# Output projection, mixing, both norms and modulation token tile by token tile, row broadcasts beside the head norm, and six attention projections inside the rwkv scan

## The reference

```
u = LN(x) * (1 + scale1) + shift1
h = u @ w_in                      # columns split into the groups of three mixers
y = concat[ RWKV-7 both ways (4 heads x 64),
            differential attention with rotary q, k (4 heads, q/k 2x64, v 128),
            HGRN2 both ways (4 heads x 64) ] @ w_out
x = LayerNorm(alpha * x + gate1 * y)
x = LayerNorm(alpha * x + gate2 * PEER(LN(x) * (1 + scale2) + shift2))
```

## Time and profile before

| | us |
|---|---|
| median of 3 runs | 6208.47 (6203.03 to 6233.56) |
| the profiled execution | 6228.09 |
| its span, first to last instruction | 6226.5 |

### The profile page before, as it was taken

The page is one execution under the profiler, slowest core; times in us unless marked ns, Lnnn a source line. Parts: engine busy times, 40 slices in busy tenths (PEclk is TensorE's granted clock), DMA queues, the critical chain, the costliest instruction groups (busy, mean ns, idle before and its releaser), DMA issues.

```text
span 6226.5 us, 64675 instructions
## 1 busy us (share of the span) xinstructions
PE 5310.1 (85%) x22991; PEld 3572.5 (57%) x22991; DVE 3707.7 (60%) x8308; ACT 1464.0 (24%) x3638; POOL 1473.6 (24%) x1540
## 2 busy tenths in 40 slices
PE   8899888786787799999999589987796846999997
PEld 3699644554663455555555379944473745666664
DVE  1545252744886688887665465416373697775665
ACT  1100021312276412112111210003221165111111
POOL 0000000000024555445553000000000036434552
PEclk9899989678897799999999789998757956999998
DMA  6000000001357899999997100010001438999996
GB/s 219 21 1 1 24 17 27 8 20 62 119 197 274 346 418 414 401 405 404 399 413 299 49 4 1 1 37 7 31 1 42 141 123 328 415 418 412 417 417 272
DMA packets 292960, 1184.08 MB, mean 190 GB/s; under 512 B 24736, under 2 KB 106912, under 8 KB 207392
## 3 DMA queue, kind: packets, MB, share of 16 engines
q0 software_dynamic: 92160, 671.13, 26.4%
q1 hardware_dynamic: 194864, 455.59, 20.0%
q10 hardware_dynamic: 5616, 53.23, 2.1%
HBM read 1130.57 MB, written 49.28 MB: 189 GB/s over the span
## 4 chain that ended last, share of the span: by engine, by line
PE 65%; DVE 18%; DMA 10%; ACT 3%; issue 2%; POOL 2%; ACTq 0%; SPq 0%; DVEq 0%; POOLq 0%
PE psum L510 64%; DMA arena<-in_ut 6%; DVE arena L1376 3%; DMA arena<-gate_blocks 2%; DMA x_tokens<-in_uv,arena 1%; DVE arena L1706 1%; DVE arena L1515 1%; DVE arena L1781 1%; DVE arena L1385 1%; DMA arena<-in_uv,arena 1%; DVE arena L1513 1%; ACT arena L1001 1%; DVE arena L1379 1%; DVE arena L1587 1%; ACT y_features L1077 1%
## 5 line engine op out<-in xcount | busy, mean ns | idle before, releaser
L510 PE MATMUL psum<-arena 128*128 128x64 f32 (+7 forms) x8416 | 1550.1, 361 | 46.0 <-DVE arena L1706 23.9
L510 PE MATMUL psum<-u_features,weight_ring 128*128 128x256 f32 (+2 forms) x4672 | 1319.7, 439 | 36.7 <-ACT arena L1106 18.3
L510 PEld LDWEIGHTS psum<-arena 128*128 128x128 f32 (+2 forms) x8416 | 1082.8, 213 | 397.3 <-issue 279.5
L510 PEld LDWEIGHTS psum<-u_features,weight_ring 128*128 128x128 f32 x4672 | 896.7, 194 | 454.4 <-issue 240.0
L1354 POOL TENSOR_TENSOR arena<-consts 128x1 f32<-128x1 f32 x640 | 334.9, 523 | 1264.4 <-DVE y_features L1610 1092.3
L510 PE MATMUL psum<-u_features,arena 128*128 128x384 f32 (+1 forms) x2048 | 588.1, 442 | 39.3 <-DMA arena<-in_ut 35.6
L1001 ACT ACTIVATE arena<-psum 128x512 f32<-128x512 f32 (+5 forms) x404 | 250.6, 620 | 1543.1 <-PE psum L510 1313.2
L510 PE MATMUL psum<-weight_ring,consts 128*128 128x512 f32 x1280 | 570.3, 592 | 0.0
L510 PEld LDWEIGHTS psum<-u_features,arena 128*128 128x128 f32 x2048 | 396.7, 195 | 253.9 <-issue 56.5
L1355 POOL DMA_INDIRECT arena<-in_uv,arena x350 | 485.3, 1387 | 99.3 <-POOL arena L1354 93.5
L1112 ACT ACTIVATE arena<-arena 128x1 f32<-128x1 f32 x640 | 129.8, 203 | 1485.4 <-DVE arena L1602 1482.3
(11 more groups left out here) (201 smaller groups left out, 5437.2 us busy)
## 6 DMA issues: line engine op xcount, KB each, us to landing
weight_ring<-in_ws SPq DMA_DIRECT2D x250, 512.0 KB, 3.6
weight_ring<-in_ut SPq DMA_DIRECT2D x128, 512.0 KB
weight_ring<-in_uv SPq DMA_DIRECT2D x128, 512.0 KB
arena<-in_ut SPq DMA_DIRECT2D x128, 512.0 KB
arena<-in_uv SPq DMA_DIRECT2D x128, 512.0 KB
gate_blocks<-arena ACTq DMA_DIRECT2D x20, 2048.0 KB, 7.8
arena<-gate_blocks SPq DMA_DIRECT2D x32, 768.0 KB, 18.9
arena<-gate_blocks SPq DMA_DIRECT2D x32, 512.0 KB, 27.2
```

The lines of the kernel that those rows point to most:

```text
L510: return pe.matmul(o, w, x, start=first, stop=last, skip_group_check=True)
```

## The change

There are two parts.

**Attention pieces in the scan.** In pass i of the rwkv scan, 12 of the 14 filler slots no longer hold three identity matmuls but a part of the q/k projection of piece i: eight slots with one matmul of 128x512 (the latent tokens, into PSUM bank 3), and four with two matmuls of 128x256 (the context, into bank 7). ACT copies both results out in the same pass. Six of eight pieces are done so, and two remain in `project`. Their targets QA and KA can't lie in the arena during the scan, so they now lie in X. The tokens in X are overwritten by that and loaded again during the hgrn stage: in layer 0 from the inputs, in layer 1 from x_kept, where ACT stores them at the start of the layer.

**The tail of the mixers.** The rows of gate1 and of mod2 (the shift and scale of the second modulation) are broadcast right after the hgrn scan, during the head norm. Four of the eight pieces of w_out stay in the ring, the other four are loaded into the arena once the hgrn scan has left it, so that PE can project all 1024 columns of one tile before it goes to the next. Mixing, both norms, transposes and modulation follow tile by tile, with two PSUM buffers for the projection and two for the transposes. The first two query pieces, which need only the first two tiles, stand ahead of the last tile's transposes.

The diff, cut to its core:

```diff
-        QA, KA = take(4 * T), take(4 * T)
+        QA, KA = X[:, 0:4 * T], X[:, 4 * T:8 * T]
...
+        WO2 = [take(PIECE) for _ in range(WO // 2)]
+        G1 = [take(D) for _ in range(2)]
+        BC = [take(D) for _ in range(4)]
...
+                    if n == tokens_back_at(l) + WO // 2:
+                        for d in range(2):
+                            sp.wait_ge(*at("hgrn state", l, NT - 1, d))
+                        for c in range(WO // 2):
+                            sp.dma_start(WO2[c], a["ws"][pieces_before(DEPTH) + l * (WO // 2) + c]).then_inc(SEM["second_half_in"], 16)
...
+                    if n == tokens_back_at(l):
+                        sp.wait_ge(*at("attn scores", l, BH * len(tiles(l)) - 1, 1))
+                        if l == 0:
+                            load_tokens("x_again")
+                        else:
+                            sp.wait_ge(SEM["x_spilled"], 16 * 2 * l)
+                            sp.dma_start(X[:, CT * D:NT * D], a["x_kept"][:, CT * D:NT * D]).then_inc(SEM["x_again"], 16)
...
+            def between(l, i, g):
+                if g < KB:
+                    w = piece_ready() if g == 0 else piece_now()
+                    ins = mm(bank(3), w[:, g * P:(g + 1) * P], xt(g, CTX, T), g == 0, g == KB - 1)
...
+                elif g < KB + KB // 2:
+                    w = piece_now()
+                    for k in (2 * (g - KB), 2 * (g - KB) + 1):
+                        ins = mm(bank(7, 0, CTX), w[:, k * P:(k + 1) * P], xt(k, 0, CTX), k == 0, k == KB - 1)
...
+                else:
+                    pe.wait_ge(*at("attn latent copied", l, i))
+                    keep_warm(bank(3, 0, P), WARM)
...
+            def out_tile(l, n, t):
+                if n >= 2:
+                    pe.wait_ge(*at("mixed", l, n - 2))
...
+            def turn_tile(l, n, t):
+                if n >= 2:
+                    pe.wait_ge(*at("ln2 modulated", l, n - 2))
+                pe.wait_ge(*at("ln2 normed", l, t))
+                for k in range(KB):
+                    b = 4 + 2 * (n % 2) + k // 4
+                    ins = pe.transpose(bank(b, (k % 4) * P, (k % 4 + 1) * P), XN[:, t * D + k * P:t * D + (k + 1) * P], ident)
...
-                        keep_warm(bank(3, 0, P), WARM)
+                        between(l, i, 2 * lev)
...
-                        keep_warm(bank(3, 0, P), WARM)
+                        between(l, i, 2 * lev + 1)
+                    pe.wait_ge(*at("attn copied", l, i))
...
-                project(l, "attn", AQK)
+                project(l, "attn", AQK, NT)
...
+                for s in streams:
+                    broadcast(l, "gate1", [16], s, 2 * s)
+                broadcast(l, "mod2", [24, 32], 0, 4)
...
+                pe.wait_ge(*at("mod2 kept", l, streams[-1]))
                 pe.wait_ge(*at("hgrn y", l))
...
+                for n, t in enumerate(ts):
+                    out_tile(l, n, t)
+                    if n:
+                        turn_tile(l, n - 1, ts[n - 1])
...
+                    act.wait_ge(*at("attn latent", l, i))
+                    copy(x[:, CTX:T], bank(3), "attn latent copied", l, i)
+                    act.wait_ge(*at("attn context", l, i))
+                    copy(x[:, 0:CTX], bank(7, 0, CTX), "attn copied", l, i)
...
+                for t in ts:
+                    stats(l, "mix", [t], SQM)
+                    stats(l, "ln2", [t], SQM)
...
+                for n, t in enumerate(ts):
...
+                    tt(xn, PS[:, 1024 * (n % 2):1024 * (n % 2) + D], G1[s], ALU.mult)
+                    stt(x, x, ALPHA, xn, ALU.mult, ALU.add, "mixed", l, n)
...
+                    if n:
+                        tile_modulated(l, n - 1, ts[n - 1])
+                    normed(l, "mix", [t], lambda t: XN[:, t * D:(t + 1) * D])
...
+                    if t == ts[-1]:
+                        for i in range(len(FETCHED[l]) - 1):
+                            fetched_input(l, i)
+                    normed(l, "ln2", [t], lambda t: XN[:, t * D:(t + 1) * D])
+                fetched_input(l, len(FETCHED[l]) - 1)
+                tile_modulated(l, len(ts) - 1, ts[-1])
```

More of the change, by code:

```diff
@@ L542, in ada_turned, with project @@
                 done(ins, *name)
-            def project(l, what, count):
-                for c in range(count):
+            def project(l, what, count, first=0):
+                for c in range(first, count):
                     w = piece_ready()
-                    if c >= 2:
+                    if c >= first + 2:
                         pe.wait_ge(*at(what + " copied", l, c - 2))
@@ L580, in query_piece @@
                 w = piece_ready()
+                if part == 0 and c < 2:
+                    pe.wait_ge(*at("ln2 modulated", l, 1))
+                    pe.wait_ge(*at("mixed", l, len(tiles(l)) - 2 + c))
+                elif part == 1 and c == 0:
+                    pe.wait_ge(*at("peer input", l))
                 if c >= 2:
@@ L1049, in scores_kept @@
                 act.wait_ge(*at("scores", l, part, c))
+                if part + c == 0:
+                    act.wait_ge(*at("fetched inputs", l))
+                    act.wait_ge(*at("ln2 turned", l, len(tiles(l)) - 1))
                 for t in ts if c == 0 else ():
@@ L1114, in slot_weight, with rows_kept @@
                         "slot weight", l, i)
[L1116 to L1121 removed]
+            def rows_kept(l, what, b, dsts, s):
+                act.wait_ge(*at(what + " rows", l, s))
+                for n, dst in enumerate(dsts):
+                    copy(dst, PS[:, 512 * b + 1024 * n:512 * b + 1024 * n + D])
+                marks[(what + " kept", l, s)] = (SEM["scalar_steps"].name, done.n)
             act.wait_ge(SEM["consts_loaded"], 48)
@@ L1327, in _ @@
                 rsqrt(HM, "hgrn norm", l)
-                for what in ("mix", "ln2"):
-                    for t in ts:
+                for t in ts:
+                    for what in ("mix", "ln2"):
                         rsqrt(ST[:, 16 + t:17 + t], what, l, t)
@@ L1852, in _ @@
                 tt(HO, HO, HG, ALU.mult, "hgrn y", l)
-                dve.wait_ge(*at("gate1 kept", l, 1 if l + 1 < DEPTH else 0))
-                for half in range(2):
-                    dve.wait_ge(*at("out projected", l, half))
-                    for n, t in enumerate(ts):
-                        c = slice(half * 512, half * 512 + 512)
-                        y = XN[:, t * D:(t + 1) * D][:, c]
-                        tt(y, bank(n), BC[1 if t < CT else 0][:, c], ALU.mult)
-                        stt(x_tile(t)[:, c], x_tile(t)[:, c], ALPHA, y, ALU.mult, ALU.add, "mixed", l, half)
-                        marks[("mix input", l, t)] = marks[("mixed", l, half)]
@@ L1863, in _ @@
-                normed(l, "mix", ts, lambda t: XN[:, t * D:(t + 1) * D])
-                dve.wait_ge(SEM["ln_rows_loaded"], 64 * l + 32)
-                for t in ts:
-                    xn = XN[:, t * D:(t + 1) * D]
-                    tt(xn, xn, LNR[0], ALU.mult)
-                    tt(x_tile(t), xn, LNR[1], ALU.add, "ln2 input", l, t)
-                normed(l, "ln2", ts, lambda t: XN[:, t * D:(t + 1) * D])
-                dve.wait_ge(*at("mod2 kept", l, 1 if l + 1 < DEPTH else 0))
-                dve.wait_ge(*at("out projected", l, 1))
@@ L1880, in _ @@
+                fetched_input(l, len(FETCHED[l]) - 1)
+                marks[("fetched inputs", l)] = ("vector_steps", done.n)
+                tile_modulated(l, len(ts) - 1, ts[-1])
+                marks[("peer input", l)] = marks[("ln2 modulated", l, len(ts) - 1)]
                 for kind, n, c in openings[l][0]:
@@ L1991 @@
         ln.append(np.stack([g["ln1_w"][l], g["ln1_b"][l], g["ln2_w"][l], g["ln2_b"][l]]))
+    pieces += [token_pieces(g["w_out"][l][:, 512:1024]) for l in range(DEPTH)]
     cf, cb = constants()
```

140 lines of the change are left out of this document (89 added, 51 removed).

## The result

The changed kernel takes 6005.67 us (median of 4 runs, 6002.42 to 6016.94). The kernel before, run beside it, takes 6221.02 (6203.03 to 6239.21). The ratio is **0.9663**, 95% interval 0.9636 to 0.9689. The forecast was 6009 in a range of 5945 to 6075. The profiled execution of after took 6002.42 us (span 6000.6) against 6228.09 of before: 225.7 us less, where the sum said 199.

The account below looks back on a forecast made before the run. PE and DVE taking turns bound the changed stages, with PE's list setting the rwkv pass. 93 (attention pieces) + 64 + 42 (tails of layers 0, 1) - 0.5 = 199 us off the median 6208.5 gives 6009, range 5945 to 6075.

Parts of the forecast that it names:

- Projection, −62.2 a layer: q/k projection after the rwkv scan: six of eight pieces leave, 62.2 us less a layer, about 22 instead of 84.6.
- Cost of the longer fillers, +15.6 a layer: rwkv scan: wider fillers in 12 slots are paid in full, 2.6 us a pass, 15.6 for six passes.
- its half-clock stretch as long as now: Sign in the rwkv scan: a pass takes 71 to 72 us and its time at half clock stays unchanged.
- the scan's clock gets better: Rival: fillers streaming more columns end the rwkv pass's half-clock time, 3.5 us a pass, 41 more, 5968 us; chance 0.10.
- PE waiting for ACT before the W product: rwkv scan: ACT's two extra copies stay covered; if not, about 1.02 us a pass, +12 for twelve passes.
- Busy time and the clock: Weighed under the better-clock rival: whether sustained busy time opens PE's clock gate; by that rule the rival is worth nothing.
- Copies on ACT, the second fetch of X, the store: Extra ACT copies and refetching X in the hgrn stage cost nothing; storing x_kept at layer 1's start costs 0.5 us.
- Broadcasts, 0 or +9.4: Layer 0 head norm: six groups take 11.3 us at full clock, 22.7 at half; 0 or 9.4 us late, 0 taken.
- Tile cycle 16.7, first tile 14.5: Tail of the mixers: DVE with its hand-overs sets 16.7 us a tile, 14.5 the first; PE needs 14.7.
- Third query piece, −64 and −42: Tail: the third query piece starts as good as 64 us earlier in layer 0 and 42 in layer 1.
- some 10 us: Tail: PE finishes the first two query pieces, then waits about 10 us before the last tile's turn.
- Later stages shift as a block: All later stages, opening and dense loop, are unchanged and only move earlier, with no change of their length.

Follow-up runs that it names:

- e1_wide: Kernel before with one 128x512 identity matmul instead of three 128x128 in 12 of 14 rwkv filler slots, no projection moved; 6210.38 us, one run, against 6220.10.
- e2_four: Kernel before with four 128x128 identity matmuls instead of three in the same 12 rwkv filler slots; 6208.81 us, one run, against 6220.10.
- e3_part2: Changed kernel with the attention pieces in the scan undone, old fillers back, new tail kept; 6124.36 us against 6220.10 of the kernel before, ratio 0.9858.
- D: Experiment with four filler doses in the changed kernel's hgrn scan, timed from the hgrn stage's own token projection to head norm; 5942.34 to 5989.49 us.
- h3_mixed: Changed kernel with hgrn fillers of two times 256 columns in the scan's first pass and 256 in the others, instead of 128; 5970.20 us, ratio 0.9596.
- h0_none: Changed kernel without any filler in the hgrn scan's levels; 5942.34 us, one run.
- h1_hgrn256: Changed kernel with one 256-column filler instead of one of 128 in each hgrn scan slot; 5989.49 us, ratio 0.9611.
- h2_hgrn512: Changed kernel with two 256-column fillers instead of one of 128 in each hgrn scan slot; 5989.27 us, one run.

## Why the prediction was right, step by step

The number came out closer than the working was. The forecast of 6009 starts from 6208.47, the median of three runs; from 6221.02, with which the result was compared, the same 199 us give 6022, 16 above the 6005.67. And two errors of opposite sign are in it: the scans were 39.6 us better than their term, the later stages 15.0 worse than nothing. That 3 us were left is luck; the terms of the projection and the tail are not.

- **Projection, −62.2 a layer: right.** −63.6 and −62.5. The window is 22.00 us against a forecast of "about 22".
- **Cost of the longer fillers, +15.6 a layer: the term that failed.** The scans came out at −5.9 and −2.5. The filler itself was priced nearly right: where both kernels have the stretch, a pass went from 69.13 to 71.09, +1.96 against +2.6. What was wrong is "its half-clock stretch as long as now": in after most passes have none, and one without is 3.3 us shorter (71.09 and 67.78). The rival "the scan's clock gets better" named this at 3.5 us a pass and had 0.10. It came true for six of ten passes of after and not for the first of a scan. e1_wide and e2_four show that clean passes come with the columns alone, and e3_part2, with the old fillers, has none. Why some passes stay unclean is open.
- **PE waiting for ACT before the W product: none, right.** In a clean pass of after PE waits 0.3 us for ACT in all, as it did in before.
- **Busy time and the clock.** The changed kernel's hgrn pass above has PE busy 35.46 of 36.87 us at 0.54, and with 512 columns in the same slots the scan holds 0.98 and 0.99. The Trainium skill ("TensorE: Matmul & The Clock Gate", Part 1), whose rule the prediction weighed there, says that a sustained busy while opens the gate. The traces do not agree, as far as the profile's busy time is that busy: it is nearly without a gap in that pass and without one in the earlier trace rows, and half is granted in both.
- **Copies on ACT, the second fetch of X, the store: nothing, right.** The clean pass of after equals that of e1_wide, which has none of them.
- **Broadcasts, 0 or +9.4: 0, right.** 10.95 us for 96 records at the full clock; the forecast had 11.3.
- **Tile cycle 16.7, first tile 14.5: right.** Norms end at 1313.82, 1330.91, 1347.61, 1364.32 and 1381.03. One modulation takes 409 ns in the group below, where 0.41 was carried on from 256 and 512 columns. It is the group by form of DVE from 1313 to 1401 (count, busy us, mean ns, idle before):

```profile
L1482 DVE TENSOR_SCALAR u_features<-psum,mod_cols 128x128 f32<-128x128 f32 x40 | 16.4, 409 | 1.5
```

- **Third query piece, −64 and −42: −64.7 and −42.2.** The wait before the last turn, "some 10 us", is 12.46 and 9.95.
- **"Later stages shift as a block": not quite.** The stages from the v projection to the head norm lost 7.1 us in layer 0 and the rest 4.3 and 3.8. Of the 7.1, 5.9 lie in the hgrn scan's part (277.4 against 271.5 us, measured as in D). In the ten profiled executions with the filler of 128 columns that part takes 271.5 to 286.3 us in layer 0, at clocks of 0.64 to 0.70, and 271.5 to 297.9 in layer 1, at 0.58 to 0.70. So 5.9 is within what the same code varies, and the "−0.2" of layer 1 compares two executions that both had the slow end. But all four with part 1 took at least 277.4 and 297.8, and most of the other six less; whether part 1 has a share in that, no run separates. The 4.3 and 3.8 are also about what kernels with the code of before vary there (2102.6 to 2108.1 us in layer 0, 2108.9 in after; 1383.8 to 1398.3 in layer 1, 1387.7 in after). No cause was shown for them.
- The sum of 199 against 226 in the profiles is the scan (39.6 more) less what was given back (15.0), and 2.6 us more from the projection and the tail. The medians differ by 215: before's profiled execution lies 7 us above its median and after's 3 below.

## What to carry over

A filler is work. Before it is tuned for the clock, take it out and look which engine is late then: in the hgrn scan that gave 65 us against the changed kernel (one run), where the best dose of fillers gave 37. In the rwkv scan the fillers were never taken out, so what they are worth there is open. In the rwkv scan, real products cost what fillers of the same columns cost (67.78 and 67.76 us a clean pass). A term that rests on the clock staying as it is needs both ends in the sum. The measured version that beats both kernels with an interval is h3_mixed at 5970; h0_none at 5942 rests on one run.

## What the runs showed of the hardware that I had not expected

- The same pass of the same program takes 64.90 us at a clock of 1.00 or 97.19 at 0.63, within one execution.
- PE can be busy without a gap and stay at half: 41.06 of 41.06 us at 0.51 in the first hgrn pass of h1_hgrn256. No wait kept the clock down there, and 512 columns in the slots of h3_mixed shortened that level loop from 41.17 to 31.31 us, though they are more work (the windows of h1_hgrn256, then the chain of h3_mixed).

```profile
1083.94:1125.00 41.06, 41.06 (x194) 28.54 (x193) 26.56 (x99) 8.81 (x11) 0.00 (x0) 0.51 0.00 1
```
```profile
1074.29 31.31 PE psum L537 x224
```

- A full clock is no end in itself: h2_hgrn512 holds 0.98 and 0.99 in the hgrn scan and needs 24 to 26 us a layer more there than h0_none at 0.60.
